# Gate units of the attention slots moved forward by one slot, and an exponential of a constant after the last key

## The chip, the core and the metric

The program runs on one core of one Trainium2 chip. The metric is the time of one execution on the device, in microseconds (us); the median of several runs is compared. The engines of a core have their own instruction queues and work in parallel: TensorE (PE in the profile, its weight loads PEld), VectorE (DVE), ScalarE (ACT), GpSimd (POOL) and SyncE (SP, which issues most of the DMAs here). Within one queue the instructions go in the order written; between queues, semaphores make one engine wait for another.

## What is computed

One layer of a decoder is applied to a prompt of 1024 tokens and to 8 sampled sequences of 8 tokens (64 rows). The part that matters here, from the reference:

```
xn = RMSNorm(x)
z  = xn @ w_in     columns = [u | v | q | k | v_attn | gate_a | gate_b]
branch A: u, v = gelu(.); v <- RMSNorm(v); f = tril(W_s[g]) v_chunk + b[g]; a = u * f
branch B: q, k RMS-normed per head, partial rotary; dilated sliding-window attention,
          3 groups x 4 heads, head_dim 64; the 3 group outputs are combined per position
merge: m = sigmoid(gate_a) * (a @ w_proj_a) + sigmoid(gate_b) * (b @ w_proj_b);  x = x + m @ w_out
x = x + HMoE(RMSNorm(x)): top-1 of 4 expert groups, then top-2 of 8 SwiGLU experts
```

The weights and activations are f32. A dense product is made of three products of a high and a low half (`three`, lines 809 to 811): high by high, high by low, low by high.

## The kernel before

**Stages.** The input projection `w_in` is cut into 25 blocks of 256 columns. Blocks 0 to 16 (attention values, v, u, q and k) are worked off in dense units, one after another. The last six of them are q and k: 54 units, one for each block and each of 9 tiles of tokens (`qk`). For each of these, TensorE makes the product (`tok_unit`), ScalarE squares it and takes a root (L1358, L1360), VectorE scales, applies the norm weight and the rotary part (`qk_norm`, L1648 to L1663), TensorE transposes the result (`qk_transposes`, L914), and ScalarE writes the transposed tile to qT or kT (`qk_evac`, L1324 and L1326). TensorE issues the transposes of unit i - 3 behind the product of unit i, so three pairs of transposes are left over once the last product is issued; GpSimd stores some of the normed keys to the outputs.

**Attention slots.** The 48 gate units (blocks 17 to 24, eight blocks of six units) are not worked off in a row but dealt out as dense filler over the slots of the attention, a loop of 72 slots (`for sl in range(S_END)`) that every engine walks through in its own queue. In slots 0 to 23 TensorE does `scores(sl)` (L943, L958), `p_transposes(sl - 1)` (L967) and `pv(sl - 2)` (L983) of the prompt; from slot 25 it does the sampled sequences: `k_transposes` (L999), `s_scores` (L1014, L1020), `s_pv` (L1046), `s_tail` (L1033, L1035), the last of these in slot 51. At the end of each slot comes one gate unit, `gate_mm(sl)`, of 24 products of 384 or 320 columns (L809 to L811). From slot 48 on, its place is taken by `branch_a`, the product of a with `w_proj_a`.

**What a slot waits for.** There is one pair of PSUM banks for the scores (6 and 7), so `scores(sl)` waits until ScalarE has taken the exponentials of the slot before (`prompt_exp`, L1402), which in turn wait for the row maxima of VectorE (`prompt_max`, L1728 to L1736). The same holds for the samples: `s_scores(m)` waits for `sample_exp(m - 1)` (L1423), which waits for `sample_max` (L1764). The first `scores` waits besides for all 54 transposed q and k tiles (semaphore `qk_T`). The gate units alternate between PSUM banks 1 and 2; gate unit g waits until unit g - 2 has been read (the first two wait for q and k units that were in the same banks). ScalarE reads gate unit sl - 1 at the head of its slot sl (`evac`, L1368: a tanh), and GpSimd stores it to `gate_scratch`.

**Other work in the slots.** In slots 2, 8, 14 and so on, the weights of the next block are split into halves (`w_hi` on ScalarE, L1297; `w_lo` on VectorE, L1586). In slots 45, 47 and 49 the stored result of branch A is split in the same way, one chunk of tokens each (`a_hi`, L1429; `a_lo`, L1786); its load waits until the gate units that still read the same buffer are done.

**Between q and k and the first slot.** Before its first `prompt_max`, VectorE waits for the stores of the keys (`k_st`) and for `qk_T`; SyncE waits for the same stores before it loads the first values (L608 to L610, then L630).

Of the kernel before, what the change touches and what calls it, by code (L numbers as in the profile page):

```python
# [25 lines left out]
ACT = mybir.ActivationFunctionType  # L26
# [127 lines left out]
def _build(nc, ctx, a, o):  # L154
    def sb(name, shape, dt=F32):
        return ctx.enter_context(nc.sbuf_tensor(name, shape, dt))
# [20 lines left out]
    eps = cst[:, CEPS:CEPS + 1]  # L177
# [130 lines left out]
    small = sb("small", [P, 8, TILES])  # L308
# [62 lines left out]
    def bank(b, n=512):  # L371
        return ps[:, b, 0:n]
# [11 lines left out]
    def s(name):  # L384
        if name not in S:
            S[name] = sem(name)
        return S[name]
# [64 lines left out]
    NGU = 6 * (NWIN - GATES0)  # L452
# [341 lines left out]
    def _(pe):  # L794
# [40 lines left out]
        def feat_unit(n, ct, c, src=None, dst=None, nk=KT):  # L835
            _, hi, lo = wslot(n)
            if ct == 0 and c == 0:
                pe.wait_ge(s("w_split"), n + 1)
            c0, w = CHUNK[c]
            src = src or xT  # L840
            out = dst if dst is not None else bank(claim(), w)
            return three(out, [lambda k, v=v: v[:, k, P * ct:P * ct + P] for v in (hi, lo)],
                         [lambda k, v=v: v[:, k, c0:c0 + w] for v in src], nk)
# [61 lines left out]
        qk = [(n, t) for n in range(11, 17) for t in range(TILES)]  # L905

        def qk_transposes(i):
            pe.wait_ge(s("qn_ready"), i + 1)
            if i >= 2:
                pe.wait_ge(s("qk_T"), i - 1)  # L910
            else:
                pe.wait_ge(s("a_ready"), 24)
            for j in range(2):
                last = tr(ps[:, 4 + i % 2, P * j:P * j + P], qn[i % 4][:, P * j:P * j + P], ident)  # L914
            last.then_inc(s("qk_tr"), 1)

        for i, (n, t) in enumerate(qk):
            tok_unit(n, t)
            if i >= 3:
                qk_transposes(i - 3)  # L920
        for i in range(len(qk) - 3, len(qk)):
            qk_transposes(i)

        def gate_mm(g_):

            if g_ < 2:
                pe.wait_ge(s("freed_dve"), 2 * NG * TILES - 3 + g_)
            else:
                pe.wait_ge(s("freed_act"), freed_g0 + g_ - 1)
            n, ct, c = units[GU0 + g_]  # L930
            feat_unit(n, ct, c, dst=bank(1 + g_ % 2, CHUNK[c][1])).then_inc(s("unit_mm"), 1)

        def scores(n):
            g, j = divmod(n, NTILE)
            nb = nblk(n)
            if n >= 1:
                pe.wait_ge(s("attn_exp"), n)
            else:
                pe.wait_ge(s("qk_T"), 2 * NG * TILES)
            sc = ps[:, 6:8, 0:2 * nb * P].rearrange("p b (h k) -> p b h k", k=nb * P)  # L940
            mask = cbf[:, BPAIR:BPAIR + P] if g == 2 else cbf[:, BPO + (2 - nb) * P:BPO + 2 * P]
            for b in range(2):
                mm(ps[:, 6 + b, 0:2 * nb * P].rearrange("p (h k) -> p h k", k=nb * P), identb,  # L943
                   mask.unsqueeze(1).to_broadcast([P, 2, nb * P]), start=True, stop=True)
            for i in range(2):
                pr = 2 * g + i
                for part in range(2 if g == 2 else nb):
                    for b in range(2):
                        q = qT[64 * b:64 * b + 64, pr, :]
                        k = kT[64 * b:64 * b + 64, pr, :]  # L950
                        if g == 2:
                            r = 2 * j + part
                            half = slice(64 * part, 64 * part + 64)
                            out, qa, ka = sc[half, b, i, half], q[:, r:NPROMPT:16], k[:, r:NPROMPT:16]
                        else:
                            out = sc[:, b, i, part * P:part * P + P]
                            qa, ka = qcols(q, g, j, 0), qcols(k, g, j, part - nb + 1)
                        last = mm(out, qa, ka, start=False, stop=True, skip_group_check=True)  # L958
            last.then_inc(s("attn_s"), 1)

        def p_transposes(n):
            nb = nblk(n)
            pe.wait_ge(s("attn_exp"), n + 1)
            if n >= 1:
                pe.wait_ge(s("attn_pt"), n)
            for i in range(NH * nb):
                last = tr(pair(4)[:, i, :], Eb[n % 2][:, i // nb, (i % nb) * P:(i % nb) * P + P], ident)  # L967
            last.then_inc(s("attn_tr"), 1)

        def pv(n):  # L970
            g, j = divmod(n, NTILE)
            nb = nblk(n)
            pe.wait_ge(s("attn_pt"), n + 1)
            pe.wait_ge(s(f"vg_in{n % 2}"), vg_count(n))
            if n >= 2:
                pe.wait_ge(s("attn_o"), n - 1)
            else:
                pe.wait_ge(s("freed_dve"), 2 * NG * TILES)
            for sl in range(NH):
                head = 2 * (sl % 2) + sl // 2  # L980
                for kb in range(nb):
                    k = 0 if g == 2 else 2 - nb + kb
                    last = mm(ps[:, 3 * (n % 2), HD * head:HD * head + HD], Pt[n % 2][:, nb * sl + kb, :],  # L983
                              vg[n % 2][:, k, HD * head:HD * head + HD], start=(kb == 0), stop=(kb == nb - 1))
            last.then_inc(s("attn_pv"), 1)
# [4 lines left out]
        def k_transposes(n):  # L990
            g, b = divmod(n, NB)
            pe.wait_ge(s(f"kc_in{n % 2}"), cache_count(n, 2, 0))
            if n >= 1:
                pe.wait_ge(s("sk_T"), n)
            else:
                pe.wait_ge(s("attn_pt"), NU)
            for hp in range(2):
                for i in range(SKT[g]):
                    last = tr(ps[:, 4 + hp, P * i:P * i + P], kc[n % 2][:, i, P * hp:P * hp + P], ident)  # L999
            last.then_inc(s("sk_tr"), 1)  # L1000
# [36 lines left out]
        def s_pv(n):  # L1037
            g, b = divmod(n, NB)
            pe.wait_ge(s("sattn_pt"), n + 1)
            pe.wait_ge(s(f"vc_in{n % 3}"), cache_count(n, 3, 1))  # L1040
            if n >= 1:
                pe.wait_ge(s("sattn_o"), n)
            tiles = list(range(SKT[g])) + [4]
            for i in tiles:
                for hd in range(NH):
                    last = mm(ps[32 * hd:32 * hd + 32, 3, P:P + HD], PTs[n % 2][:, i, 32 * hd:32 * hd + 32],  # L1046
                              vc[n % 3][:, i, HD * hd:HD * hd + HD], start=(i == 0), stop=(i == 4), skip_group_check=True)
            last.then_inc(s("sattn_pv"), 1)
# [30 lines left out]
                  [lambda k, v=v: v[:, k, c0:c0 + w] for v in bT], 2).then_inc(s("b_mm"), 1)  # L1079

        gate_mm(0)
        for sl in range(S_END):
            if sl < NU:
                scores(sl)
            if 1 <= sl <= NU:
                p_transposes(sl - 1)
            if 2 <= sl < NU + 2:
                pv(sl - 2)
            m = sl - S_SAMPLE
            if -1 <= m < NSU - 1:  # L1090
                k_transposes(m + 1)
            if 0 <= m < NSU:
                s_scores(m)
            if 2 <= m < NSU + 2:
                s_pv(m - 2)
            if 1 <= m <= NSU:
                s_tail(m - 1)
            for step, i in comb_step(sl):
                if step == 3:
                    b_transposes(i)  # L1100
            if 1 <= sl < NGU:
                gate_mm(sl)
            elif sl >= NGU:
                branch_a(sl - NGU)
            if S_B <= sl < S_B + 8:
                branch_b(sl - S_B)
# [169 lines left out]
    def _(act):  # L1276
        act_ = nc.scalar.activation
# [38 lines left out]
        def qk_evac(k):  # L1316

            act.wait_ge(s("qk_tr"), k + 1)
            g, t = divmod(k, TILES)
            src = ps[:, 4 + k % 2, 0:GW].rearrange("p (a b) -> p a b", b=P)  # L1320
            full, samp = (qT, qTs) if g < NG else (kT, kTs)
            g %= NG
            if t == ST:
                act_(samp[:, 2 * g:2 * g + 2, :], src[:, :, 0:NSAMP], ACT.Copy).then_inc(s("qk_T"), 1)  # L1324
            else:
                act_(full[:, 2 * g:2 * g + 2, P * t:P * t + P], src, ACT.Copy).then_inc(s("qk_T"), 1)  # L1326
# [62 lines left out]

        for j in range(6 * TILES - 3, 6 * TILES):  # L1390
            qk_evac(j)
        for j in range(4):
            act.wait_ge(s(f"v_st{j}"), 16 * vst_n[-1][j])

# [894 lines left out]
```

## Time and profile before

| | us |
|---|---|
| median of 3 runs | 1757.91 |
| lowest and highest of these | 1756.33, 1759.67 |
| the profiled execution | 1759.51 |
| its span in the trace | 1757.7 |
| busy in the span: TensorE | 1659.7 (94%) |
| VectorE | 1016.3 (58%) |
| ScalarE | 775.7 (44%) |
| GpSimd | 311.0 (18%) |
| mean granted TensorE clock | 0.975 of full speed |

The trace gives for each instruction its start, its length, its engine and line, and, where the engine sat idle before it, how long and what ended the idle time. The granted clock is a share of 2.4 GHz: 1.00 is full speed, 0.50 is 1.2 GHz. Matmuls overlap, so the time of a row of them is read from the start of one to the start of the next and not from the sum of the lengths.

### The profile page before, as it was taken

Reading aid. Unit: us, or ns where it says so; the run is one execution under the profiler, and the core shown is the slowest. Engines: PE = TensorE matmul, PEld = TensorE weight load, DVE = VectorE, ACT = ScalarE, POOL = GpSimd, SP = SyncE. Lnnn points to the kernel's source line nnn. Section 1 sums busy time; section 2 is a strip of 40 time slices with the busy share of each in tenths; the row PEclk is TensorE's granted clock in tenths of the full one; section 3 lists DMA queues with packets and bytes.
Section 4 is the critical chain, followed back from the end, with each engine's and each line's share of the span. In section 5 each row is a group of like instructions: output and inputs, shape, how many; then the busy total and the mean of one; then the engine's idle time right before and its main releaser. Section 6 shows DMA issues by size and latency. Waiting matters only on the chain.

```text
span 1757.7 us, 27924 instructions
## 1 busy us (share of the span) xinstructions
PE 1659.7 (94%) x11000; PEld 1502.4 (85%) x11000; DVE 1016.3 (58%) x1432; ACT 775.7 (44%) x1038; POOL 311.0 (18%) x346
## 2 busy tenths in 40 slices
PE   5999999999989999999999899699999999999990
PEld 5999999999979999988999788578888888888870
DVE  5312412277754333233565423689999899898975
ACT  5222211133333333233311122378777787878860
POOL 0000301000011112211011400023333333333310
PEclk9999999999989999999999999799999999999995
DMA  5312523221323223465843322689999999999967
GB/s 191 125 66 99 182 78 134 82 85 61 110 92 111 87 90 103 132 197 181 300 137 108 112 72 73 245 317 378 378 377 373 373 376 401 390 387 383 389 237 311
DMA packets 124026, 365.70 MB, mean 208 GB/s; under 512 B 20225, under 2 KB 80193, under 8 KB 97714
## 3 DMA queue, kind: packets, MB, share of 16 engines
q1 hardware_dynamic: 103346, 312.77, 48.8%
q0 software_dynamic: 19344, 46.99, 7.3%
q10 hardware_dynamic: 1232, 4.46, 0.7%
q8 instruction: 77, 1.26, 0.3%
q14 instruction: 27, 0.22, 0.0%
HBM read 330.41 MB, written 68.52 MB: 227 GB/s over the span
## 4 chain that ended last, share of the span: by engine, by line
PE 91%; DVE 4%; DMA 3%; ACT 1%; issue 1%; POOL 0%; SPq 0%; DVEq 0%; POOLq 0%; ACTq 0%
PE ps L809 14%; PE ps L811 14%; PE ps L810 14%; PE ps L1211 6%; PE ps L1213 6%; PE ps L1212 6%; PE ps L1234 3%; PE ps L1236 3%; PE ps L1235 3%; PE ps L983 2%; PE ps L1131 2%; PE ps L1133 2%; PE ps L1200 2%; PE ps L1132 2%; PE ps L958 2%; DMA part<-expert_out_scratch 1%
## 5 line engine op out<-in xcount | busy, mean ns | idle before, releaser
L809 PE MATMUL ps<-part,part 128*128 128x256 f32 (+2 forms) x1784 | 556.4, 312 | 12.1 <-DVE part L1842 7.3
L811 PE MATMUL ps<-part,part 128*128 128x256 f32 (+2 forms) x1784 | 543.2, 304 | 0.0
L810 PE MATMUL ps<-part,part 128*128 128x256 f32 (+2 forms) x1784 | 543.0, 304 | 0.0
L2049 DVE TENSOR_TENSOR part<-part,part 128x2048 fp32r<-128x2048 f32 x192 | 438.9, 2292 | 54.4 <-ACT part L1498 49.1
L1498 ACT ACTIVATE part<-part 128x2048 fp32r<-128x2048 f32 x192 | 368.4, 1920 | 123.8 <-PE ps L1213 87.4
L809 PEld LDWEIGHTS ps<-part,part 128*128 128x128 f32 x1784 | 341.7, 192 | 16.6 <-DVE part L1842 9.3
L810 PEld LDWEIGHTS ps<-part,part 128*128 128x128 f32 x1784 | 342.2, 192 | 0.0
L811 PEld LDWEIGHTS ps<-part,part 128*128 128x128 f32 x1784 | 341.6, 191 | 0.0
L1211 PE MATMUL ps<-part,part 128*128 128x512 f32 x512 | 204.1, 399 | 4.5 <-DVE part L2055 3.5
L1213 PE MATMUL ps<-part,part 128*128 128x512 f32 x512 | 200.7, 392 | 0.0
L1212 PE MATMUL ps<-part,part 128*128 128x512 f32 x512 | 200.3, 391 | 0.0
L1586 DVE TENSOR_TENSOR part<-part,part 128x2048 fp32r<-128x2048 f32 x34 | 77.9, 2291 | 118.2 <-ACT part L1297 118.2
L1211 PEld LDWEIGHTS ps<-part,part 128*128 128x128 f32 x512 | 97.1, 190 | 26.1 <-DVE part L2055 4.1
L1213 PEld LDWEIGHTS ps<-part,part 128*128 128x128 f32 x512 | 96.7, 189 | 21.0
L1212 PEld LDWEIGHTS ps<-part,part 128*128 128x128 f32 x512 | 96.8, 189 | 19.0
L1234 PE MATMUL ps<-part,part 128*128 128x512 f32 x256 | 103.2, 403 | 1.9 <-DVE part L2063 1.9
L1236 PE MATMUL ps<-part,part 128*128 128x512 f32 x256 | 100.6, 393 | 0.0
L1235 PE MATMUL ps<-part,part 128*128 128x512 f32 x256 | 100.6, 393 | 0.0
L2224 POOL DMA_INDIRECT part<-xn_scratch,idxc x29 | 79.9, 2755 | 25.2 <-POOL idxc L2221 25.2
L1728 DVE TENSOR_REDUCE stat<-ps 128x4 f32<-128x512 f32 (+1 forms) x24 | 22.5, 936 | 106.5 <-PE ps L958 106.5
L1368 ACT ACTIVATE part<-ps 128x384 f32<-128x384 f32 (+1 forms) x48 | 22.7, 474 | 137.4 <-PE ps L811 137.4
L2161 POOL DMA_DIRECT2D gate_scratch<-part x48 | 26.5, 552 | 284.0 <-ACT part L1368 277.8
(247 smaller groups left out, 2120.4 us busy)
## 6 DMA issues: line engine op xcount, KB each, us to landing
part<-w_gate SPq DMA_DIRECT2D x64, 1024.0 KB, 8.2
part<-w_up SPq DMA_DIRECT2D x64, 1024.0 KB, 7.4
part<-w_down SPq DMA_DIRECT2D x64, 1024.0 KB, 7.4
part<-w_in SPq DMA_DIRECT2D x25, 1024.0 KB, 5.2
part<-x_prompt SPq DMA_DIRECT2D x16, 512.0 KB, 3.6
part<-expert_out_scratch SPq DMA_DIRECT2D x8, 1024.0 KB, 10.1
gate_scratch<-part POOLq DMA_DIRECT2D x32, 192.0 KB, 2.8
part<-gate_scratch SPq DMA_DIRECT2D x4, 1088.0 KB, 8.5
```

Of the source, the lines that this page charges most:

```text
L809: mm(out, lhs[0](k), rhs[0](k), start=(k == 0), stop=False)
L810: mm(out, lhs[0](k), rhs[1](k), start=False, stop=False)
L811: last = mm(out, lhs[1](k), rhs[0](k), start=False, stop=(k == n - 1))
L1211: mm(bank(2 + j % 2), xgh[:, kk, :], hi[:, k, :], start=(kk == 0), stop=False)
L1212: mm(bank(2 + j % 2), xgh[:, kk, :], lo[:, k, :], start=False, stop=False)
L1213: last = mm(bank(2 + j % 2), xgl[:, kk, :], hi[:, k, :], start=False, stop=(kk == KT - 1))
L1234: mm(bank(5 + half), hTh[:, kk, :], hi[:, k, cols], start=(kk == 0), stop=False)
L1235: mm(bank(5 + half), hTh[:, kk, :], lo[:, k, cols], start=False, stop=False)
L1236: last = mm(bank(5 + half), hTl[:, kk, :], hi[:, k, cols], start=False, stop=(kk == 3))
L1498: act_(ehi[:, off % NSPL, :], eraw[:, off % NRAW, :], ACT.Copy).then_inc(s("e_hi"), 1)
L2049: tt(elo[:, off % NSPL, :], eraw[:, off % NRAW, :], ehi[:, off % NSPL, :].bitcast(F32), ALU.subtract)\
L2224: pool.indirect_dma_start(xg, None, xn_d, bass.IndirectOffsetOnAxis(ap=idxc[:, 0:1], axis=0), bounds_check=T - 1, oob_is_err=False).then_i ...
```

## The change

Three edits, two on TensorE's queue and one on ScalarE's:

```
@@ TensorE
             tok_unit(n, t)
             if i >= 3:
                 qk_transposes(i - 3)
-        for i in range(len(qk) - 3, len(qk)):
-            qk_transposes(i)
...
         gate_mm(0)
+        for i in range(len(qk) - 3, len(qk)):
+            qk_transposes(i)
         for sl in range(S_END):
...
-            if 1 <= sl < NGU:
-                gate_mm(sl)
+            if sl + 1 < NGU:
+                gate_mm(sl + 1)
             elif sl >= NGU:
                 branch_a(sl - NGU)
@@ ScalarE
         for j in range(6 * TILES - 3, 6 * TILES):
             qk_evac(j)
+        act_(small[:, 7, 0:1], eps, ACT.Exp)
         for j in range(4):
             act.wait_ge(s(f"v_st{j}"), 16 * vst_n[-1][j])
```

Gate unit 0 goes ahead of the last three pairs of transposes. Slot 0, which had no gate unit, gets unit 1, each following slot the unit that stood in the next one, and slot 47 is left without one. The number of instructions on TensorE is the same. The tile small[:, 7] is read by nothing. The new line of ScalarE shifts the lines below it by one, and the moved loop shifts those of TensorE between by two.

TensorE, where the q and k units end and the slots begin. part_88, part_89, part_86 and part_87 are the normed tiles of units 50 to 53, part_102 is a tile of exponentials, part_54 the high half of the gate weights. Before:

```order
L914 MATMUL ps<-cst,part_88 128x128 x2
L914 MATMUL ps<-cst,part_89 128x128 x2
L914 MATMUL ps<-cst,part_86 128x128 x2
L914 MATMUL ps<-cst,part_87 128x128 x2
L809 MATMUL ps<-part_49,part_54 128x384
...
L943 MATMUL ps<-cbf 128x256 x2
L958 MATMUL ps<-part_85,part_84 128x128 x4
L943 MATMUL ps<-cbf 128x512 x2
L958 MATMUL ps<-part_85,part_84 128x128 x8
```

Now:

```order
L914 MATMUL ps<-cst,part_88 128x128 x2
L809 MATMUL ps<-part_49,part_54 128x384
...
L914 MATMUL ps<-cst,part_89 128x128 x2
L914 MATMUL ps<-cst,part_86 128x128 x2
L914 MATMUL ps<-cst,part_87 128x128 x2
L941 MATMUL ps<-cbf 128x256 x2
L956 MATMUL ps<-part_85,part_84 128x128 x4
L809 MATMUL ps<-part_49,part_54 128x384
...
L941 MATMUL ps<-cbf 128x512 x2
```

A gate unit now stands between the transposes of units 50 and 51, and another between the first and the second scores, where nothing stood.

TensorE, slots 47 and 48, at the end of the gate units (128x320 is gate unit 47, 128x384 with part_54 the first unit of branch A). Before:

```order
L999 MATMUL ps<-cst,part_110 128x128 x4
...
L1033 MATMUL ps<-cst,part_126 128x128 x2
L1035 MATMUL ps<-cst,part_126 8x128
L809 MATMUL ps<-part_49,part_52 128x320
...
L999 MATMUL ps<-cst,part_111 128x128 x4
...
L1035 MATMUL ps<-cst,part_127 8x128
L809 MATMUL ps<-part_49,part_54 128x384
```

Now:

```order
L997 MATMUL ps<-cst,part_110 128x128 x4
...
L1031 MATMUL ps<-cst,part_126 128x128 x2
L1033 MATMUL ps<-cst,part_126 8x128
L997 MATMUL ps<-cst,part_111 128x128 x4
...
L1033 MATMUL ps<-cst,part_127 8x128
L809 MATMUL ps<-part_49,part_54 128x384
```

The attention work of slot 48 now follows that of slot 47 with no dense unit between.

ScalarE, where the last keys are written (part_83 is kTs, the keys of the samples). Before and now, as one difference:

```order
 L1326 ACTIVATE part_85<-ps 128x2x128 x3
 L1324 ACTIVATE part_83<-ps 128x128
-L1402 ACT_TABLE_LOAD
-L1402 ACTIVATE part_102,part_96<-ps,nm 128x128 x4
-L1368 ACTIVATE part_106<-ps 128x384
```

```order
L1324 ACTIVATE part_83<-ps 128x128
L1392 ACT_TABLE_LOAD
L1392 ACTIVATE small<-cst 128x1
L1403 ACTIVATE part_102,part_96<-ps,nm 128x128 x4
L1368 ACTIVATE part_106<-ps 128x384
```

The load of ScalarE's function table, which stood directly ahead of the first exponentials, now stands ahead of the new small instruction.

## Rows read from the trace of the kernel before

**Rows 1.** Page, part 4: the chain that ended last, by engine

```profile
PE 91%; DVE 4%; DMA 3%; ACT 1%; issue 1%; POOL 0%; SPq 0%; DVEq 0%; POOLq 0%; ACTq 0%
```

**Rows 2.** Windows, TensorE: stretch, its length, busy (instructions), granted clock, DMA share, GB/s

```profile
508.00:511.00 3.00, 0.84 (x8) 1.00 0.34 131
511.00:513.00 2.00, 0.69 (x2) 0.53 0.19 70
533.00:963.00 430.00, 430.00 (x3615) 1.00 0.45 148
964.00:966.00 2.00, 0.00 (x0) 1.00 0.00 0
985.00:992.00 7.00, 5.32 (x25) 0.54 0.53 119
```

**Rows 3.** Timeline of TensorE, 508 to 535 (start, length, line, count, idle before)

```profile
508.24 0.60 PE L914 MATMUL ps<-cst,part 128*128 128x128 f32 x4
511.18 0.69 PE L914 MATMUL ps<-cst,part 128*128 128x128 f32 x2 [2.34 <-DVE part L1663]
513.03 0.69 PE L914 MATMUL ps<-cst,part 128*128 128x128 f32 x2 [1.16 <-DVE part L1663]
513.37 0.67 PE L809 MATMUL ps<-part,part 128*128 128x384 f32 x1
...
519.74 0.39 PE L943 MATMUL ps<-cbf 128*128 128x256 bf16 x2
...
524.85 1.03 PE L943 MATMUL ps<-cbf 128*128 128x512 bf16 x2 [4.07 <-ACT part L1402]
...
527.82 0.80 PE L967 MATMUL ps<-cst,part 128*128 128x128 f32 x4
528.38 0.42 PE L809 MATMUL ps<-part,part 128*128 128x384 f32 x1
...
532.65 0.61 PE L943 MATMUL ps<-cbf 128*128 128x512 bf16 x2
...
534.28 1.09 PE L967 MATMUL ps<-cst,part 128*128 128x128 f32 x8
```

**Rows 4.** Timeline of ScalarE, 509 to 523

```profile
509.52 0.64 ACT L1326 ACTIVATE part<-ps 128x256 f32<-128x256 f32 x2
...
513.75 0.28 ACT L1324 ACTIVATE part<-ps 128x128 f32<-128x128 f32 x1 [1.46 <-PE ps L914]
521.99 1.28 ACT L1402 ACT_TABLE_LOAD   x1 [7.96 <-DVE nm L1736]
```

**Rows 5.** Timeline of VectorE, 512 to 522

```profile
512.78 0.19 DVE L1663 TENSOR_TENSOR part<-part,part 128x32 f32<-128x32 f32 x1
520.92 0.69 DVE L1728 TENSOR_REDUCE stat<-ps 128x4 f32<-128x512 f32 x1 [7.95 <-PE ps L958]
```

**Rows 6.** Waits of SyncE's queue, 495 to 560, and its timeline there

```profile
SPq L610 <- DMA out_sample_k_w<-part: 5.8, 1, 5.8
```

```profile
516.57 28.99 SPq L630 DMA_DIRECT2D part<-v_scratch  x7
```

**Rows 7.** Timeline of TensorE, slots 47 to 49

```profile
843.40 0.60 PE L999 MATMUL ps<-cst,part 128*128 128x128 f32 x4
...
845.47 0.39 PE L809 MATMUL ps<-part,part 128*128 128x320 f32 x1
...
849.07 0.60 PE L999 MATMUL ps<-cst,part 128*128 128x128 f32 x4
...
855.41 0.29 PE L1014 MATMUL ps<-cbf 128*128 128x256 bf16 x2
```

**Rows 8.** Timelines of ScalarE and VectorE, the same slots

```profile
845.93 2.76 ACT L1429 ACTIVATE part<-part 128x3072 fp32r<-128x3072 f32 x1
...
852.65 0.48 ACT L1423 ACTIVATE part<-ps,snm 128x264 f32<-128x264 f32 x1 [2.35 <-DVE snm L1767]
```

```profile
848.73 3.36 DVE L1786 TENSOR_TENSOR part<-part,part 128x3072 fp32r<-128x3072 f32 x1 [2.24 <-ACT part L1429]
```

More of the change, by code:

```diff
@@ L920, in _ @@
                 qk_transposes(i - 3)
-        for i in range(len(qk) - 3, len(qk)):
-            qk_transposes(i)
         def gate_mm(g_):
@@ L1081, in _ @@
         gate_mm(0)
+        for i in range(len(qk) - 3, len(qk)):
+            qk_transposes(i)
         for sl in range(S_END):
@@ L1100, in _ @@
                     b_transposes(i)
-            if 1 <= sl < NGU:
-                gate_mm(sl)
+            if sl + 1 < NGU:
+                gate_mm(sl + 1)
             elif sl >= NGU:
@@ L1391, in _ @@
             qk_evac(j)
+        act_(small[:, 7, 0:1], eps, ACT.Exp)
         for j in range(4):
```

## The prediction

> **What bounds the kernel now.** I read the chain of work that ended last first: TensorE holds 91% of it, so what moves the time is TensorE's own idle time and its clock [rows 1]. The windows then show where either is to be had. From 533 to 963 us, through nearly all the attention slots, TensorE has 430.00 busy us out of 430.00 at the full clock [rows 2]: there nothing can be gained but by less work. The reader is to look just ahead of that stretch, in TensorE's timeline [rows 3]. Between the last dense unit and the third scores it idles three times: 2.34 and 1.16 us for the normed keys of the last two units, and 4.07 us for the first exponentials. Behind the first idle stretch the granted clock is 0.53 [rows 2], which is the 1.2 GHz level for most of the window.
>
> **The sum before.** I cut one piece out of TensorE's queue, from the start of the transposes at 508.24 to the start of the third scores at 532.65: 24.41 us [rows 3]. It holds four pairs of transposes, gate units 0 and 1, two scores and one set of transposed exponentials. Its parts: 7.57 us idle; gate unit 0 takes 519.74 - 513.37 = 6.37 us, half of it slow, against 532.65 - 528.38 = 4.27 us for unit 1 at the full clock; the second scores take 527.82 - 524.85 = 2.97 us against 534.28 - 532.65 = 1.63 us for the same work one slot on [rows 3].
>
> **Part 1: gate unit 0 ahead of three pairs of transposes.** It needs unit 50 scaled by VectorE, not transposed, and that is long done. So it can start behind the transposes of unit 50, at some 508.4, and ends at 508.4 + 4.27 = 512.7. Of the three pairs, those of units 51 and 52 are ready by then; the last unit is normed at 512.78 + 0.19 = 512.97 [rows 5]. All three are thus at hand together, and what is late next is ScalarE: the third pair reuses a bank and waits until unit 51 is written out. Two such evictions took 0.64 us [rows 4], and from the issue of a pair to its eviction passed 513.75 - 513.03 = 0.72 us at the slow clock [rows 3, 4], perhaps 0.4 at the full one. So: first eviction at 513.1, third pair at 513.4 to 513.5, last eviction at 513.9 and done by 514.2. Before, the last eviction was done at 513.75 + 0.28 = 514.03 [rows 4]. I put the first scores at 514.3; they started at 519.74. Idle time left: about 1 us in two bits, beside 3.50 before.
>
> **Part 2: gate unit 1 in slot 0.** Its PSUM bank is free. The first scores took 519.74 to 524.85 - 4.07 = 520.78 with their tail, so unit 1 starts at 515.3 and ends at 519.6. In its shade lies the chain to the first exponentials. VectorE's maxima would start at 515.5, but here a wait comes up that nothing showed before: VectorE, like SyncE, waits for the stores of the keys, and SyncE's queue was held by the last of them for 5.8 us and went on at 516.57 [rows 6]. Before, VectorE started its maxima only at 520.92 and that wait was covered [rows 5]. Now it sets the start: 516.6. From there to ScalarE's table load passed 521.99 - 520.92 = 1.07 us, and from the table load to the second scores 524.85 - 521.99 = 2.86 us, of which 1.28 are the load [rows 3 to 5]. Without the load: 516.6 + 1.07 + 1.58 = 519.2, just inside the cover of unit 1, by 0.3 us.
>
> **Part 3: the small exponential.** It adds one instruction on one column and moves the table load of 1.28 us to 514.2, where ScalarE idled for 7.96 us [rows 4]. Its own cost is nothing on the path: both are over 1 us before the maxima. Without it the exponentials would end at 520.5 and TensorE would idle some 0.9 us; that is its worth here, not the whole 1.28.
>
> **The sum at the start.** Second scores at 519.6; + 1.63 for them, + 528.38 - 527.82 = 0.56 for the transposed exponentials, + 4.27 for gate unit 2 [rows 3]: third scores at 526.0 against 532.65, with one gate unit more behind them. Gain: 6.6 + 4.27 = **10.9 us**.
>
> **Slots 2 to 46.** Each still has one gate unit, now the next one, and TensorE stays full. A gate unit now waits for a tanh one ScalarE slot later than it did. ScalarE reads at the head of its slot what TensorE finished a whole slot earlier, and GpSimd's stores of the gates only come sooner. Cost: nothing, if ScalarE isn't late (rival D). The weights of the next block are split in slots 2, 8 and so on, and wanted three slots later instead of four. Nothing.
>
> **Slot 47 without a gate unit: a new wait.** Before, slot 47 began at 843.40, its gate unit ran from 845.47 to 849.07 = 3.60 us, slot 48's attention work takes the same 845.47 - 843.40 = 2.07 us, and slot 49 began at 855.41 [rows 7]. Now, in the same clock: slot 48 at 845.5, branch A's first unit at 847.5, done at 847.5 + 4.27 = 851.8. Slot 49 then wants the scores of the last sample, which wait for the exponentials before them. These come at 852.65 + 0.48 = 853.1, behind the splitting of a chunk of a: 2.76 us on ScalarE from 845.93 and 3.36 us on VectorE from 848.73, ahead of the row maxima in VectorE's queue [rows 8]. None of this hung on gate unit 47, so it doesn't come sooner. TensorE idles 853.1 - 851.8 = **1.3 us**. The bounds are 0, if the loads bring the split forward, and 3.60, the whole cover; I take 1.3, since it is built from the very rows. Behind it, the eviction and the loads for branch A keep their place relative to TensorE.
>
> **Total.** 10.9 - 1.3 = **9.6 us less**. The profiled execution, 1759.51 (span 1757.7), would go to 1749.9. The median of the runs lies 1.6 us lower, and I forecast it: 1757.9 - 9.6 = **1748.3**. All later stages start on what TensorE finishes, none by a time of its own, so I count the shift in full.
>
> **The clock, row and page.** After 2.34 us without a matmul the clock was at 0.53, and over 964 to 966 us, also empty, it stayed at 1.00 [rows 2]: the length of a gap alone doesn't tell. The Trainium skill (TensorE: Matmul & The Clock Gate, "Part 1: The HAM clock gate") says that long gaps bring the half rate, and that the point at which it changes varies from run to run, since it depends on where a free-running count stands. The pair of rows agrees with the second half. By the first half alone the new gaps, none near a microsecond and a half, would be safe and the time 1748.3.
>
> **Rivals.**
> A (0.67), the forecast: 1748.3, by itself 1745 to 1751.5. The width is the clock: from 985 to 992 us it was at 0.54 with 5.32 us busy [rows 2], which costs up to 3 us and may vanish or turn up elsewhere once everything stands elsewhere.
> B (0.14): the thin stretch from 512.7 to 515.3 takes the clock down all the same. Gate unit 1 then costs what unit 0 did, 6.37 - 4.27 = 2.1, or scores as well, 2.97 - 1.63 = 1.3: 1750.4 to 1751.7. For it speaks the 2.34 us gap, against it that over half of the new stretch is work.
> C (0.09): a bigger wait than I count. The whole of gate unit 47 was cover (2.3 more), or the last key store lands later and VectorE with it (0.3 us are free, then each is paid): 1750.6 to 1753.
> D (0.04), slower: the gate units get stuck behind ScalarE. Each now waits for a tanh that stands in ScalarE's queue behind the exponentials, weight splits and chunk splits of the slot before. The place is slots 1 to 46; it decides from 9.6 / 46 = 0.2 us a slot, and at half a microsecond the time would be 1757.9 - 9.6 + 23 = 1771. Against it: the longest such piece starts 845.93 - 843.40 = 2.5 us into its slot and takes 2.76; the slot before branch A is 5.67 us long and a gate unit comes 2.07 us into the next [rows 7, 8]. That leaves some 2 us after the tanh.
> E (0.06), no change: TensorE comes to a later point sooner and waits there for a transfer, or the moved instructions don't run where they stand. Near 1757. The full 430 us between speak against it.
>
> **How the numbers follow.** About 0.2% (3.5 us) is what a measurement of this kernel can tell from no change. A, B and nearly all of C lie below 1754.4: faster 0.90. E gives same 0.06, D slower 0.04. The range takes A with its clock, B, and C's larger part: 1744.8 to 1752.8.
>
> **What would show it.** Right: the first scores near 514.3 and a gate unit on both sides of them; the table load within 2 us behind the last key; VectorE's first maxima held until about 516.6, more than 1 us after the scores; the third scores at 526; no idle TensorE until slot 49, and there 1.3 us for sample exponentials. Wrong: a clock under 0.9 in 515 to 525 (B), gate units waiting for the tanh (D), idle time in the slots between, or more than 1.3 us in slots 48 and 49 (C).

## The result, and the profile after

| | us |
|---|---|
| before, median of 7 runs (lowest, highest) | 1759.26 (1756.33, 1759.67) |
| changed, median of 7 runs (lowest, highest) | 1751.99 (1750.62, 1755.49) |
| ratio of the runs, 95% interval | 0.9968 (0.9958 to 0.9978) |
| span of the profiled execution: before, changed | 1757.7, 1748.8 |

By the ratio the change makes the kernel faster by 0.32%, some 5.6 us (3.9 to 7.4 by the interval); the two medians lie 7.3 us apart, at the upper end of that, and I go by the ratio. Forecast were 9.6 us. The sign and the place of the gain were right, and it was little more than half as large.

TensorE's timeline where the q and k units end, in the changed kernel. It answers to [rows 3]:

```profile
506.92 0.38 PE L914 MATMUL ps<-cst,part 128*128 128x128 f32 x2
507.06 0.42 PE L809 MATMUL ps<-part,part 128*128 128x384 f32 x1
...
511.33 0.60 PE L914 MATMUL ps<-cst,part 128*128 128x128 f32 x4
512.28 0.41 PE L914 MATMUL ps<-cst,part 128*128 128x128 f32 x2 [0.35 <-ACT part L1326]
513.05 0.39 PE L941 MATMUL ps<-cbf 128*128 128x256 bf16 x2 [0.37 <-ACT part L1324]
513.38 0.72 PE L956 MATMUL ps<-part,part 64*128 64x128 f32 x8
514.02 0.45 PE L809 MATMUL ps<-part,part 128*128 128x384 f32 x1
...
518.30 0.61 PE L941 MATMUL ps<-cbf 128*128 128x512 bf16 x2
...
524.61 0.61 PE L941 MATMUL ps<-cbf 128*128 128x512 bf16 x2
```

Of 7.57 us of idle time, 0.72 are left, in the two bits that the prediction named. The gate unit between the transposes takes 511.33 - 507.06 = 4.27 us, that is the full clock. From the transposes of unit 50 to the third scores it is 524.61 - 506.92 = 17.69 us against 24.41, with one gate unit more in it: 6.72 + 4.27 = **11.0 us gained** (forecast 10.9).

ScalarE and VectorE in the same place, answering to [rows 4, 5]:

```profile
512.72 0.28 ACT L1324 ACTIVATE part<-ps 128x128 f32<-128x128 f32 x1 [0.32 <-PE ps L914]
513.02 1.28 ACT L1392 ACT_TABLE_LOAD   x1
514.31 0.20 ACT L1392 ACTIVATE small<-cst 128x1 f32<-128x1 f32 x1
515.32 0.37 ACT L1403 ACTIVATE part<-ps,nm 128x128 f32<-128x128 f32 x1 [0.81 <-DVE nm L1737]
...
516.71 0.50 ACT L1368 ACTIVATE part<-ps 128x384 f32<-128x384 f32 x1
```

```profile
514.24 0.69 DVE L1729 TENSOR_REDUCE stat<-ps 128x4 f32<-128x512 f32 x1 [2.58 <-DMA out_sample_k_w<-part]
```

The wait for the store of the keys is there: it is what released VectorE. But the store had been issued at 511.95 and was down 2.2 us later, less than 0.1 us behind the scores (513.38 + 0.72 = 514.10). The exponentials end at 516.7, and gate unit 1 runs until 518.3: a cover of 1.6 us to spare, not 0.3.

Then slots 46 to 49, answering to [rows 7]; the first column is the start, the bracket idle time and its releaser:

```profile
829.75 0.60 PE L997 MATMUL ps<-cst,part 128*128 128x128 f32 x4
...
835.42 0.60 PE L997 MATMUL ps<-cst,part 128*128 128x128 f32 x4
...
841.17 0.66 PE L997 MATMUL ps<-cst,part 128*128 128x128 f32 x4 [3.44 <-DMA part<-cache_k_w]
...
843.80 0.67 PE L809 MATMUL ps<-part,part 128*128 128x384 f32 x1
...
849.10 0.29 PE L1012 MATMUL ps<-cbf 128*128 128x256 bf16 x2
```

Here is where the prediction failed. Slot 47 begins at 835.42 and its attention work ends 2.07 us later, at 837.5. Slot 48 opens with the transposes of the last sample's keys, and these keys are still in transfer: TensorE stands until 841.17. The first product of branch A behind the gap takes 849.10 - 843.80 = 5.30 us instead of 4.27, since its first matmuls run at half the clock. From slot 47 to slot 49 it is 13.68 us. Before it was 12.01, of which 3.60 were the gate unit; 8.41 would have been left. So **5.3 us are lost here**, where 1.3 were forecast.

ScalarE and VectorE in these slots, answering to [rows 8]:

```profile
840.22 2.76 ACT L1430 ACTIVATE part<-part 128x3072 fp32r<-128x3072 f32 x1 [2.16 <-DMA part<-a_scratch]
...
846.95 0.48 ACT L1424 ACTIVATE part<-ps,snm 128x264 f32<-128x264 f32 x1 [3.15 <-DVE snm L1768]
```

```profile
843.02 3.36 DVE L1787 TENSOR_TENSOR part<-part,part 128x3072 fp32r<-128x3072 f32 x1 [4.50 <-ACT part L1430]
```

Before, ScalarE began to split the chunk of a 2.5 us after the start of slot 47 (845.93 - 843.40). Now it waits for the load and begins 4.8 us after it (840.22 - 835.42), so the exponentials end 12.0 us after the start of slot 47 and not 9.7. TensorE doesn't wait for them, since the wait for the keys has held it up longer.

The waits of TensorE over 495 to 1000 us in the changed kernel (total, times, longest):

```profile
PE ps L997 <- DMA part<-cache_k_w: 4.0, 2, 3.4
```

The second of these two waits, 0.6 us, is in one of the sample slots ahead of slot 47. The account by stages, from the two traces:

| stage | before | after | after, per work |
|---|---|---|---|
| transposes of unit 50 to third scores | 24.41 | 17.69, one gate unit of 4.27 more | -11.0 |
| third scores to slot 47 | 310.75 | 310.81, a gate unit of 3.60 for one of 4.27 | +0.7 |
| slots 47 and 48 | 12.01 | 13.68, a gate unit of 3.60 less | +5.3 |
| sum | | | -5.0 |

This sum of 5.0 us agrees with the ratio (3.9 to 7.4). The spans differ by 8.9, near the forecast of 9.6 only by chance: one profiled execution against one other also carries 1.3 us from ahead of the place (508.24 against 506.92) and 2.6 us from behind slot 49, where nothing was changed. Over the traces of this case the stretch from slot 49 to the end went from 899.7 to 902.8 us.

### The profile page after: what moved, and what is told of

Its sections match the earlier page's. It is cut to its first block, busy times and chain, and to the rows that moved or that the text cites. A ratio compares the mean times of both kernels' runs of the same rounds, so it can differ in the third digit from the quotient of the medians.

```text
span 1748.8 us, 27925 instructions
## 1 busy us (share of the span) xinstructions
PE 1655.7 (95%) x11000; PEld 1499.8 (86%) x11000; DVE 1016.3 (58%) x1432; ACT 771.4 (44%) x1039; POOL 310.2 (18%) x346
## 4 chain that ended last, share of the span: by engine, by line
PE 89%; DMA 4%; DVE 4%; ACT 1%; issue 1%; SPq 1%; POOL 0%; DVEq 0%; POOLq 0%; ACTq 0%
PE ps L809 14%; PE ps L811 14%; PE ps L810 14%; PE ps L1211 6%; PE ps L1213 6%; PE ps L1212 6%; PE ps L1234 3%; PE ps L1236 3%; PE ps L1235 3%; PE ps L981 2%; PE ps L1131 2%; PE ps L1133 2%; PE ps L1200 2%; PE ps L1132 2%; PE ps L956 2%; DMA part<-expert_out_scratch 1%
## 5 line engine op out<-in xcount | busy, mean ns | idle before, releaser
L1403 ACT ACTIVATE part<-ps,nm 128x128 f32<-128x128 f32 (+1 forms) x96 | 38.6, 414 | 117.7 <-DVE nm L1737 117.7
```

## The experiments

Question: is the loss at slot 47 really what ate the gain, and what is its cause? Theory Q says that the last keys are late because they stand in SyncE's queue behind a load of 1.5 MB. Rival R says that transfers are slow there whatever stands ahead. Rival S says that the gain is given back wherever the hole is. Each ratio is against the kernel before on the same chip; the rows don't all come from one chip. The two runs on the small exponential alone, further down, were one execution each and have no ratio.

| kernel | ratio | interval |
|---|---|---|
| changed kernel | 0.9968 | 0.9958 to 0.9978 |
| load of a behind the keys | 0.9973 | 0.9961 to 0.9985 |
| empty slot 42 | 0.9938 | 0.9925 to 0.9952 |
| first edit only | 0.9971 | 0.9960 to 0.9982 |
| shift and small exponential only | 0.9987 | 0.9975 to 0.9999 |
| empty slot 46 | 0.9962 | 0.9946 to 0.9977 |
| empty slot 4 | 0.9934 | 0.9909 to 0.9960 |

### The load of a behind the last keys

```
-            if sl in (NGU - 4, NGU - 2, NGU):
-                load_a((sl - NGU + 4) // 2)
+            if sl in (NGU - 4, NGU - 1, NGU):
+                load_a({NGU - 4: 0, NGU - 1: 1, NGU: 2}[sl])
```

> The changed kernel, with one step of SyncE moved: the load of the second chunk of a (1.5 MB) is issued behind the keys of the last sample instead of ahead of them. In the changed kernel these keys landed 10.0 us after their issue, and TensorE stood 3.44 us for them in slot 48. Theory Q (the keys are late because they queue behind the chunk): that wait falls under 1 us. The split of the chunk then comes later instead, its load issued at about 833 in that trace's time, and TensorE waits 2 to 3 us in slot 49 for the exponentials behind it; slots 47 and 48 together take 12 to 13 us instead of 13.68. Rival R (the transfers of that stretch are slow whatever stands ahead, and only the 3.6 us of cover is missing): the wait in slot 48 stays at 3 us or more.

The time from issue to landing of the keys, first in the kernel before, then in the changed kernel, then in this one, for the loads whose issue falls into 828 to 840 us of each; the last keys are those issued last:

```profile
L620 SPq DMA_DIRECT2D part<-cache_k_w x4: 570/665/844, 832.3 to 839.2; - x4
...
DMA to landing us min/median/max: 6.2/7.0/7.2
```

```profile
L620 SPq DMA_DIRECT2D part<-cache_k_w x3: 582/642/2606, 825.6 to 831.1; - x3
...
DMA to landing us min/median/max: 7.6/7.8/10.0
```

```profile
L620 SPq DMA_DIRECT2D part<-cache_k_w x2: 539/574/609, 829.0 to 829.6; - x2
...
DMA to landing us min/median/max: 2.7/3.8/4.8
```

Without the chunk ahead of them, the keys are down in 4.8 us at most. TensorE's timeline of this kernel, slots 47 to 49:

```profile
834.03 0.60 PE L997 MATMUL ps<-cst,part 128*128 128x128 f32 x4
...
836.18 0.60 PE L997 MATMUL ps<-cst,part 128*128 128x128 f32 x4
...
847.93 0.28 PE L1012 MATMUL ps<-cbf 128*128 128x256 bf16 x2 [5.07 <-ACT part L1424]
```

The wait for the keys is gone, so Q holds against R. But the time didn't move (0.9973): the wait is now in slot 49, 5.07 us where I had expected 2 to 3, for the exponentials behind the split of the chunk. The chunk was issued at 832.03, took 8.4 us, and ScalarE waited for it; the chain of 2.77 and 3.36 us then ran its course. Slots 47 and 48 took 847.93 - 834.03 = 13.90 us; my 12 to 13 was a miss. Both loads want to be early, and with an attention slot of 2 us the one that goes second is late.

### The hole in slot 42, and in slot 4

```
-            if sl + 1 < NGU:
-                gate_mm(sl + 1)
+            HOLE = 42
+            if sl < HOLE:
+                gate_mm(sl + 1)
+            elif HOLE < sl < NGU:
+                gate_mm(sl)
             elif sl >= NGU:
                 branch_a(sl - NGU)
```

> The changed kernel, but the slot without a gate unit is 42 and not 47: slots 0 to 41 have the unit of the next slot, slots 43 to 47 their own, as before. If the loss stands where slot 47 lies bare (theories Q and R alike), slots 47 and 48 take 12.0 us again with no wait for keys, slot 42 costs under 0.5 us of idle time, and the kernel is 10.4 us faster than before: ratio 0.994, against 0.9968 of the changed kernel. Rival S (what the start gains is given back further on, wherever the hole is): the ratio stays at 0.9968.

Slots 42, 43 and 44 of this kernel on TensorE; the slot without a gate unit is the first:

```profile
803.87 0.60 PE L997 MATMUL ps<-cst,part 128*128 128x128 f32 x4
...
806.46 0.60 PE L997 MATMUL ps<-cst,part 128*128 128x128 f32 x4
...
813.09 0.60 PE L997 MATMUL ps<-cst,part 128*128 128x128 f32 x4
```

Slot 42 takes 2.59 us, all of it work. From slot 47 to slot 49 it is 843.46 - 831.44 = 12.02 us again. The ratio is 0.9938, that is 10.9 us less than before, and its interval lies clear of that of the changed kernel. So the whole difference between forecast and measurement hung on which slot was left empty. S falls. The run doesn't say how much of this is the cover of slot 47 and how much the loads: with the hole in 42, gate units 43 to 47 stand in their own slots again, and SyncE, whose load of the chunk waits for gate units, issues it as it did before (more on this under what stays open).

The same with the hole in slot 4, among the prompt's attention:

> The changed kernel with the hole in slot 4, among the prompt's attention. From the trace before: the attention work of slot 4 takes 4.26 us and its exponentials end 5.1 us after its start, so TensorE waits 0.9 to 1.0 us for them ahead of the scores of slot 5, and for no load. Time: 10.9 - 1.0 = 9.9 us less than before, ratio 0.9944. Against rival S (the gain is given back wherever the hole is) and with the hole in slot 42 as the comparison, which had no wait at all.

```profile
PE ps L941 <- ACT part L1406: 0.8, 1, 0.8
```

That line of the waits is the only one that the hole adds: 0.8 us for the exponentials, against 0.9 to 1.0 expected. The ratio is 0.9934, within its interval the same as with the hole in slot 42; this interval of four executions touches that of the changed kernel (0.9960 against 0.9958). By their ratios these two are the fastest kernels of the case.

### The hole in slot 46

The same edit with 46.

> The changed kernel with the hole one slot earlier, in 46. The keys that slot 47 asks for come behind a block of w_proj_a of 1 MB; in the changed kernel's trace they were issued at 828.2 at the latest and landed 7.8 us later, 836.0, and slot 47 would ask for them 2.07 us after the start of slot 46 at 829.75, so at 831.8. If the rule is that the hole costs what the key load is late by, TensorE waits some 3 to 4 us in slot 47 and the time is like the changed kernel's, ratio 0.996 to 0.997. If only the chunk of a ahead of the last keys does the harm, this is as good as the hole in slot 42: 0.994.

```profile
832.32 0.66 PE L997 MATMUL ps<-cst,part 128*128 128x128 f32 x4 [1.75 <-DMA part<-cache_k_w]
...
840.22 0.66 PE L997 MATMUL ps<-cst,part 128*128 128x128 f32 x4 [2.00 <-DMA part<-cache_k_w]
```

The time is that of the changed kernel (0.9962), as expected of the rule that a hole costs what the loads behind it are late. The details differ: I had put 3 to 4 us into slot 47, and found 1.75 there and 2.00 more in slot 48. The chunk of a ahead of the last keys is therefore not the only harm: the keys that slot 47 asked for had the block of w_proj_a ahead of them. Of the last slots only 46 and 47 were tried.

### One edit at a time

The first edit alone (from the changed kernel, the small exponential taken out and `if 1 <= sl < NGU: gate_mm(sl)` put back):

> Only the first edit: gate unit 0 ahead of the three pairs of transposes. Slot 0 is empty as before, each slot has its own gate unit, no small exponential. From the start of the transposes of unit 50: first scores at +6.1 us, VectorE's maxima at +7.3, second scores at +11.2 (with the table load on the path), third scores at +17.7 at the full clock or +19.0 with a slow stretch behind the idle one, against +24.4 before and +17.7 with one unit more in the changed kernel. Nothing lost at slot 47. So 5.4 to 6.7 us faster than before, ratio 0.9962 to 0.9969: as much as the whole change. If instead the gate units' shift brings most of the net gain, this gives 3 us or less.

```profile
508.75 0.38 PE L914 MATMUL ps<-cst,part 128*128 128x128 f32 x2
...
514.88 0.39 PE L941 MATMUL ps<-cbf 128*128 128x256 bf16 x2 [0.37 <-ACT part L1324]
...
519.99 1.03 PE L941 MATMUL ps<-cbf 128*128 128x512 bf16 x2 [4.07 <-ACT part L1402]
...
529.15 0.61 PE L941 MATMUL ps<-cbf 128*128 128x512 bf16 x2
```

First scores at +6.13, second at +11.24, as expected. Behind the idle 4.07 us the clock is slow, and longer than I had allowed for: third scores at +20.4, not +19.0, so 4.0 us gained in this trace. The ratio of 0.9971 is 5.1 us (3.2 to 7.0), just under my 5.4 to 6.7, and within the intervals as much as the whole change brings.

The other two edits alone:

```
-        gate_mm(0)
         for i in range(len(qk) - 3, len(qk)):
             qk_transposes(i)
+        gate_mm(0)
```

> The changed kernel with the first edit undone: the last three pairs of transposes come ahead of gate unit 0 again; the shift of the gate units and the small exponential stay. At the start the wait of 4.07 us ahead of the second scores and the slow clock behind it go (some 5.6 us), the two waits for the normed keys (2.34 and 1.16 us) and the slow gate unit 0 stay. At the end the 5.3 us of slots 47 and 48 are lost. Net nothing: within 1 us of the kernel before, ratio 0.9995 to 1.0005. If the gains of the two edits overlapped instead of adding up, it would be 2 to 4 us faster.

```profile
PE ps L997 <- DMA part<-cache_k_w: 3.9, 1, 3.9
PE ps L914 <- DVE part L1664: 3.8, 2, 2.3
```

The waits for the normed keys stay, the wait ahead of the second scores is gone, and the last keys are waited for. The ratio of 0.9987 (0.9975 to 0.9999) is 2.3 us faster; I had expected within 1 us. The interval allows anything from 0.2 to 4.4. Part of it shows in the trace: from the same start to the third scores it is 531.72 - 509.50 = 22.22 us, a gain of 2.2 + 4.3 = 6.5 and not 5.6, as gate unit 0 had less of the slow clock this time. The shift as it was made thus costs at its end nearly what it brings at its beginning.

### The small exponential

Taken out of the changed kernel:

> The changed kernel without the small exponential. The prediction put its worth at 0.9 us (a wait of TensorE ahead of the second scores). In the changed kernel's trace the first exponentials end at 516.7 and gate unit 1 at 518.3, so 1.28 us more would still be covered: from that trace no wait, or under 0.2 us, and a gain of nothing. Rival: the load of the table is paid in full, 1.28 us of idle time.

```profile
513.07 0.39 PE L941 MATMUL ps<-cbf 128*128 128x256 bf16 x2 [0.37 <-ACT part L1324]
...
518.31 0.61 PE L941 MATMUL ps<-cbf 128*128 128x512 bf16 x2
```

5.24 us from the first to the second scores, against 5.25 with it. It is worth nothing there. And added alone to the kernel before:

> The kernel before with the small exponential alone. There the table load lies on the path to the second scores, so TensorE's wait ahead of them falls from 4.07 to 2.8 us. Rival: the load also costs a drain or an eviction is held up, and the wait stays above 3.5 us.

```profile
523.89 0.81 PE L943 MATMUL ps<-cbf 128*128 128x512 bf16 x2 [2.78 <-ACT part L1403]
```

The wait falls from 4.07 to 2.78: the 1.28 us of the load and no more. That is read from one trace; one execution of 1759.17 us can't show 1.3 us in the time. The same instruction is worth 1.3 us where the exponentials are what TensorE waits for, and nothing once a gate unit covers them. The kernel without it also repeats the wait of slot 48 (3.96 us, in the changed kernel 3.44).

## Why the prediction was right, and where it failed

**The start (parts 1 and 2).** Right: 11.0 us against 10.9, with the idle bits, ScalarE's evictions as what is late next, and the clock as it was told. The clock stayed at 1.00 through the whole stretch, so rival B didn't come about:

```profile
508.00:526.00 18.00, 17.28 (x123) 15.20 (x123) 6.30 (x21) 7.18 (x25) 2.24 (x4) 1.00 0.19 65
```

(A window: stretch, length, busy time and count of PE, PEld, DVE, ACT and POOL, granted clock, DMA share, GB/s.) The wait for the key stores was foreseen and exists, but it was timed a microsecond too late: I took its end, 516.57, over from the trace before. The store landed in 3.1 us there and in 2.2 here, and this trace began the whole place 1.3 us earlier.

**Part 3.** Wrong in size: 0.9 us forecast, 0 measured, for the same reason. A cover that is only 0.3 us by the sum can turn out either way, and the forecast should have priced both.

**Slots 2 to 46.** Right but for 0.7 us, of which 0.6 are a first wait for sample keys. Rival D didn't occur: no gate unit waited for a tanh.

**"Slot 47 without a gate unit".** This is the step that failed: the sum put it at 1.3 us, as one wait for the exponentials in slot 49, and it measured 5.3, with the wait in slot 48 and for the last keys. It went wrong in two places.

The first is the path. The sum followed one chain, the one through the split of a chunk, and took it for the wait that ends last. The next instruction of TensorE in slot 48 was passed over: the transposes of the last keys, which wait for a transfer. In the trace before, the last of these loads was issued at 839.2 and took up to 7.2 us, so it was down at some 846.4, while TensorE was to ask at 845.5. Nobody waited for it then, for the gate unit lay over it until 849.07. The forecast's own rule was to ask of a cover that is taken away who else was under it. Reading that row would have named the wait, but not its price: 0.9 us there would have ended inside the 1.3 for the exponentials, which were due at 853.1 either way.

The second is the time of the loads, and it is the larger. The sum took it over from the trace before ("None of this hung on gate unit 47", and the loads for branch A "keep their place relative to TensorE"). They didn't keep it. The last keys were down 846.4 - 843.4 = 3.0 us after the start of slot 47 before, and 841.1 - 835.4 = 5.7 in the changed kernel; the split of the chunk began 2.5 us after it before and 4.8 now. So the chain that the sum did follow was mispriced too: its exponentials were to end 9.7 us after the start of slot 47 and ended 12.0 after it. Had the keys been there in time, TensorE would have asked for these exponentials 2.07 + 2.07 + 4.27 = 8.4 us after the start of slot 47. That makes an estimate of 3.6 us of idle time from these rows, all that the bounds allowed. The run with the two loads exchanged had the keys in time and waited 5.07 us there.

The 5.3 us are 3.44 idle for the keys plus 0.2 ahead of them, 1.0 for a slow first product of branch A and 0.6 for the attention work behind the gap, as the clock falls there to the slow level. The idle part is about the upper bound of 3.60, the length of the gate unit; the slow clock comes on top of it, and the bound had no room for that. Rival C named the whole cover, but gave it 0.09 and no cause; rival E, with 0.06, named a wait for a transfer at a later point, and that is what came, though it took half of the gain and not all. The time of 1751.99 lies in the forecast's range, which was drawn for the clock at the start, for rival B and for part of C; that it was met says nothing for the sum.

With the hole in slot 42 the loss is gone and the kernel gains 10.9 us, what the prediction's start had promised. The shortfall against the forecast is this one term.

**Clock behind a gap.** A slow stretch followed where TensorE had stood: over 835 to 850 us the granted clock was 0.89 in the changed kernel, and 1.00 with the hole in slot 42. The Trainium skill (TensorE: Matmul & The Clock Gate, "HAM oscillation — how this bites in real kernels") tells of a kernel whose matmuls start at the half rate behind each wait for a transfer. The gap of slot 48 did the same here, once, and it cost 1.0 + 0.6 us.

**What stays open.** Why the loads came later relative to slot 47. The traces narrow it down. SyncE issues the chunk once the gate units that read its buffer are done. Before, it had to wait for them (2.9 us at most for a chunk, by its list of waits); in the changed kernel each of them is done one slot earlier, no such wait is left, and the chunk goes out closer behind the 1 MB block of w_proj_a. The two issues, before and in the changed kernel:

```profile
831.86 0.40 SPq L563 DMA_DIRECT2D part<-w_proj_a  x1
...
837.91 0.39 SPq L644 DMA_DIRECT2D part<-a_scratch  x1
```

```profile
824.53 0.40 SPq L563 DMA_DIRECT2D part<-w_proj_a  x1
...
830.07 0.39 SPq L644 DMA_DIRECT2D part<-a_scratch  x1
```

The same two issues in the nine traces in which the chunk goes ahead of the last keys, in us:

| kernels | chunk issued behind the block | chunk, issue to landing | slower of the last two key loads |
|---|---|---|---|
| gate units 43 to 47 in their own slots (before, first edit only, small exponential alone, holes 42 and 4) | 6.1 | 7.5 to 8.1 | 7.2 to 7.6 |
| changed kernel | 5.5 | 10.1 | 10.0 |
| without the small exponential, shift only, hole 46 | 4.3 to 4.6 | 11.9 to 12.2 | 9.9 to 10.5 |

So the 10 us are no accident of one trace: they come with gate units 45 and 46 standing one slot early. Counted from the landing of the block the chunk needs 6.4 to 8.3 us in all ten traces, however early it is issued, which fits a chunk that queues behind the block; and the block was down 4.7 us ahead of slot 47 before, and 2.8 in the changed kernel. That is argued from the traces; no run changed the place of the block alone. The block itself took 8.1 to 9.0 us in the kernels of the lower rows and in the one with the loads exchanged, and 6.3 to 7.5 in those of the upper row, and why is open.

## What to carry to other kernels

When dense filler is moved to close one gap, another gap opens where it is taken away. List everything that lay under it, transfers first, since a load that lands late but under cover shows in no list of waits. List also the loads that are released by the filler itself: they are issued at another time once it moves, and their landing can't be taken over from the trace before. Put the hole where no large load is due: here the kernels with the hole in slot 42 or 4 gained 10.9 us or more, and those with it in 46 or 47 under 7. And price an edit by the wait that it shortens after the other edits, not before.

## What the runs showed of the hardware

The last two loads of keys, 128 KB each, took 2.7 and 4.8 us from issue to landing with the chunk of 1.5 MB issued behind them, and 6.4 to 10.5 with it right ahead of them in the same queue (nine traces). The Trainium skill (DMA: Bandwidth & Descriptors, "Queues, rings and completion order") says that each DMA engine consumes the descriptors of a ring in their order; the run with the two loads exchanged agrees.

The load of ScalarE's function table was moved here by one small instruction that needs the new table. It began 0.02 us behind the last eviction (512.72 + 0.28 = 513.00) and took 1.28 us, and the next instruction followed at once. The Trainium skill (ScalarE: Activation LUTs, "What ACT_TABLE_LOAD costs") adds a drain of 1.38 us to each switch. No such time shows in these rows, and taking the load off the path gave back 1.29 us (4.07 to 2.78), not 2.66.
